# Extra transposes of the identity in front of TensorE's waits

## What is computed

```python
# depth A (d = 1024, 256 tokens)
x = x + gate0 * retention(norm(x) * (1 + scale0) + shift0)      # 4 heads, w_in 1024x6144, w_out 2048x1024
x = x + gate1 * forgetting_attention(norm(x) * (1 + scale1) + shift1)   # 16 heads
x = rms_norm(x, final_g)
# depth B
x = layer_norm(ALPHA * x + conformer_conv(x))      # 31 taps per channel, a layer norm inside
x = layer_norm(ALPHA * x + swiglu(x))              # hidden width 2816
x = layer_norm(ALPHA * x + short_gated_conv(x))    # 3 taps
x = layer_norm(ALPHA * x + mixture_of_experts(x))  # 8 experts, top 2, hidden width 3584
```

## Time and profile before

| | |
|---|---|
| median of 3 runs | 1935.29 us (1934.23 to 1935.48) |
| the profiled execution | 1935.74 us, of which the span of its instructions is 1934.0 us |
| mean granted TensorE clock | 0.974 of full speed |
| TensorE busy with matmuls | 1803.0 us (93% of the span) |
| VectorE, ScalarE, GpSimd busy | 76%, 55%, 2% |
| HBM | 262 GB/s in the mean |

### The profile page before, as it was taken

One profiled execution on the slowest core, in us unless ns is written; L12 is line 12 of the kernel. 1 busy time (PEld: TensorE's weight loads), 2 busy tenths in 40 slices (PEclk: granted clock), 3 DMA queues, 4 the chain that ended last, 5 costly groups with the idle time before them and its releaser, 6 DMA issues.

```text
span 1934.0 us, 23674 instructions
## 1 busy us (share of the span) xinstructions
PE 1803.0 (93%) x9475; PEld 1547.6 (80%) x9475; DVE 1471.2 (76%) x1339; ACT 1062.2 (55%) x912; POOL 34.1 (2%) x34
## 2 busy tenths in 40 slices
PE   2899889988988999897999999999999999999995
PEld 2888678868978998796788887888878888888884
DVE  5686856485976554576788888889888898888895
ACT  1334234553843333232767777767677677777772
POOL 0000002000000000000000000000000000000000
PEclk9999889999999999897999999999999999999998
DMA  9588354405304547454699999999999999999992
GB/s 339 189 301 318 114 214 162 174 14 188 138 1 137 190 153 261 142 186 152 245 339 351 368 366 337 342 354 377 350 342 346 365 361 346 354 361 371 355 380 96
DMA packets 209604, 506.75 MB, mean 262 GB/s; under 512 B 6549, under 2 KB 8877, under 8 KB 209496
## 3 DMA queue, kind: packets, MB, share of 16 engines
q1 hardware_dynamic: 204832, 498.09, 70.6%
q10 hardware_dynamic: 4488, 6.58, 1.0%
q0 software_dynamic: 176, 0.53, 0.1%
HBM read 504.13 MB, written 1.05 MB: 261 GB/s over the span
## 4 chain that ended last, share of the span: by engine, by line
PE 86%; DVE 8%; ACT 2%; issue 2%; DMA 1%; POOL 1%; ACTq 0%; POOLq 0%; DVEq 0%
PE psum L692 27%; PE psum L694 26%; PE psum L693 26%; DVE R L1800 2%; PE psum L1013 2%; PE psum L1041 1%; DVE units L1457 1%; DMA ring<-in_mod_w 1%; POOL root_out L1424 1%; PE psum L1082 1%; DVE stats L1860 1%; DMA R<-in_positions 0%; DVE R L1531 0%; DVE x L1869 0%; PE psum L704 0%
## 5 line engine op out<-in xcount | busy, mean ns | idle before, releaser
L1457 DVE TENSOR_TENSOR units<-ring,units 128x2048 fp32r<-128x2048 f32 x451 | 1012.5, 2278 | 241.0 <-ACT units L1148 167.9
L1365 ACT CAST units<-ring 128x2048 fp32r<-128x2048 f32 x332 | 629.7, 1914 | 244.5 <-PE psum L694 145.9
L692 PE MATMUL psum<-units,xr 128*128 128x512 f32 x1120 | 444.1, 397 | 8.0 <-issue 4.5
L694 PE MATMUL psum<-units,xr 128*128 128x512 f32 x1120 | 438.4, 391 | 0.0
L693 PE MATMUL psum<-units,xr 128*128 128x512 f32 x1120 | 438.1, 391 | 0.0
L1148 ACT CAST units<-ring 128x2048 fp32r<-128x2048 f32 (+1 forms) x119 | 218.4, 1879 | 223.2 <-PE psum L694 187.2
L692 PE MATMUL psum<-units,H 128*128 128x512 f32 x696 | 274.6, 395 | 2.2 <-DVE H L1457 2.2
L694 PE MATMUL psum<-units,H 128*128 128x512 f32 x696 | 272.4, 391 | 0.0
L693 PE MATMUL psum<-units,H 128*128 128x512 f32 x696 | 272.4, 391 | 0.0
L692 PE MATMUL psum<-xr,units 128*128 128x256 f32 x864 | 247.1, 286 | 12.7 <-DVE units L1457 11.4
L692 PEld LDWEIGHTS psum<-units,xr 128*128 128x128 f32 x1120 | 211.6, 189 | 52.7 <-issue 7.6
(11 more groups left out here) (242 smaller groups left out, 1210.0 us busy)
## 6 DMA issues: line engine op xcount, KB each, us to landing
ring<-in_moe_w_gate SPq DMA_DIRECT2D x56, 2048.0 KB, 9.5
ring<-in_moe_w_up SPq DMA_DIRECT2D x56, 2048.0 KB, 9.4
ring<-in_moe_w_down SPq DMA_DIRECT2D x56, 2048.0 KB, 9.6
ring<-in_mod_w SPq DMA_DIRECT2D x12, 2048.0 KB, 9.9
ring<-in_ret_w_in SPq DMA_DIRECT2D x11, 2048.0 KB, 10.1
ring<-in_fox_w_in SPq DMA_DIRECT2D x8, 2048.0 KB, 8.5
ring<-in_sc_w_in SPq DMA_DIRECT2D x6, 2048.0 KB, 7.9
ring<-in_ffn_w_gate SPq DMA_DIRECT2D x5, 2048.0 KB, 8.0
```

What stands on the lines that cost most here:

```text
L692: mm(dst, left[0], right[0], start=first, stop=False)
L694: return mm(dst, left[1], right[0], start=False, stop=last)
L1365: nc.scalar.copy(*expert_unit_parts(q, j, half, 0)).then_inc(unit_high, 1)
L1457: return v.tensor_tensor(dst, src, high.bitcast(F32), ALU.subtract)
```

## The change

`repeat_ident(dst, n)` issues n transposes of the 128x128 identity (the data and the second operand are both the identity) into `dst`. The calls stand in front of waits; the target is a part of a bank that TensorE holds already and whose content the transposes or matmuls behind the wait overwrite. The description of the change speaks of thirteen places; the diff has eleven calls with a count above zero: 10 and 34 in front of heads 1 and 2 of the retention's transposes, 28 in x1T, 32 in x2T, 30 in conf_nT, 36 in front of the second tile of x3T, 38 and 30 in the two tiles of x4T, 36 in front of the second tile of x5T, 22 in front of the rank matmuls and 24 in front of the first gather. That is 320 transposes. In the retention and at the ranks `take_bank` moves ahead of the wait that it followed.

```diff
+            def repeat_ident(dst, n):
+                for _ in range(n):
+                    nc.tensor.transpose(dst, ident, ident)
+
-            def transpose_in(name, src, ready=None):
+            def transpose_in(name, src, ready=None, fill=(0, 0)):
                 banks = [take_bank(name, g) for g in range(4)]
                 for tt in range(NT):
+                    repeat_ident(banks[0][:, tt * P:(tt + 1) * P], fill[tt])
                     if ready is not None:
                         ready(tt)
...
             for h in range(RH):
-                pe.wait_ge(ret_u_ready, 2 * (h + 1))
                 for g in range(2 * h, 2 * h + 2):
                     b = take_bank("ret_uT", g)
+                    if g % 2 == 0:
+                        repeat_ident(b[:, 0:P], (0, 10, 34, 0)[h])
+                        pe.wait_ge(ret_u_ready, 2 * (h + 1))
...
-            transpose_in("x1T", xn1, lambda tt: pe.wait_ge(xn_ready, NT + tt + 1))
+            transpose_in("x1T", xn1, lambda tt: pe.wait_ge(xn_ready, NT + tt + 1), (28, 0))
...
-            transpose_in("x2T", x, lambda tt: pe.wait_ge(x_ready, tt + 1))
+            transpose_in("x2T", x, lambda tt: pe.wait_ge(x_ready, tt + 1), (32, 0))
...
-            transpose_in("conf_nT", conf_n, lambda tt: wait_emptied("conf_cT", 2 * tt + 1))
+            transpose_in("conf_nT", conf_n, lambda tt: wait_emptied("conf_cT", 2 * tt + 1), (30, 0))
...
-            transpose_in("x3T", x, lambda tt: pe.wait_ge(x_ready, NT + tt + 1))
+            transpose_in("x3T", x, lambda tt: pe.wait_ge(x_ready, NT + tt + 1), (0, 36))
...
-            transpose_in("x4T", x, lambda tt: pe.wait_ge(x_ready, NT * 2 + tt + 1))
+            transpose_in("x4T", x, lambda tt: pe.wait_ge(x_ready, NT * 2 + tt + 1), (38, 30))
...
-            transpose_in("x5T", x, lambda tt: pe.wait_ge(x_ready, NT * 3 + tt + 1))
+            transpose_in("x5T", x, lambda tt: pe.wait_ge(x_ready, NT * 3 + tt + 1), (0, 36))
...
+            b = take_bank("rank", 0)
+            repeat_ident(b[:, 0:P], 22)
             pe.wait_ge(mask_ready, 1)
-            b = take_bank("rank", 0)
...
+            repeat_ident(psum[:, 0, 0:P], 24)
             gather(0, 0)
             wide_product(0, 0, 0)
```

## The result

The changed kernel is slower: 1944.16 us median of 11 runs (1941.26 to 1945.69), against 1934.99 for the kernel before in 11 runs beside it. The ratio is 1.0045, with a 95% interval of 1.0034 to 1.0056: 6.6 to 10.8 us. The prediction was 1931.0, a gain, and its range ended at 1936.0.

A forecast was written before the change was run, and what follows sets the result against it. TensorE was taken to bound the kernel (86% of the last chain, VectorE 8%). Terms 1.1 + 1.9 + 0.3 + 0.4 + 1.15 + 0.9 + 0 - 1.5 = 4.25 us gave a median of 1931.0, range 1927.0 to 1936.0.

The forecast's parts named there:

- The experts are untouched and only start sooner: Experts' loop: no term of its own; their transfers are asked for as units come free and move with them.
- as at 1175.4: Inside the experts: starvation that comes and goes by more than 2 us, listed as a sign of being wrong.
- The head: The fills at the nine places up to x5T, without those at the ranks and the gather; terms make 6.05 us.
- Transposes hold the clock: All fills: float32 transposes alone raise TensorE's clock, as seen at x2T, though the Trainium skill says the contrary.
- x1T: Fill of 28: transposes in 1.9 instead of 3.65 us, products at the high clock; 2.6 us in full, 1.9 taken.
- x2T, conf_nT, x1T together: First three seams: gains of 0.3 for x2T, 0.4 for conf_nT (earlier start only) and 1.9 for x1T.
- x3T, x4T, x5T: Later seams: gains of 1.15, 0.9 and 0.3 us; x5T to the ranks taken as 0 altogether, its 0.3 included.
- Retention: Fills of 10 and 34: head 2 delayed 3.6 us under VectorE, products gain between 0 and 2.1; 1.1 taken.
- The ranks: Fill of 22 at the low clock, 4.7 us; x5T to the ranks between -0.5 and +1.7, 0 taken.
- The gather: Fill of 24 before the first gather: 2.0 us later, 0.5 given for the clock; term -1.5, bounds -4.6 and +0.6.
- the slower one: Rival, chance 0.08: fill before the first gather at 912.4 stays at the low clock, gather ends 4.6 us late; 1939.
- Every fill holds: Rival, chance 0.12: clock high at all fills and through L986, 11.7 us gained at most, some 9 likely; 1926.

The follow-up runs named there:

- before_pad56: The kernel before with 56 identity transposes added in a wait near the start, none at the seams: 1943.08 us, ratio 1.0050.
- before_pad72: The kernel before with 72 identity transposes added near the start, none at the seams: 1935.19 us, ratio 1.0008.

## Why the prediction was wrong

**The step that failed** is the sentence "The experts are untouched and only start sooner". Their instructions are untouched, their place in the instruction stream is not. The prediction priced the 320 transposes as time of TensorE and never as code in front of a loop. With the loop put back where it was, the same fills gave a ratio of 0.9979, 4.1 us faster (2.1 to 6.0), against the forecast of 4.25; with them taken out and only the place moved, 13.7 us were lost. The profile of before showed the clue: the idle time at 1175.40 and at 1425.80 is behind the two jumps, both put down to issue. The prediction used these for what idle time does to the clock; it listed starvation "as at 1175.4" that comes and goes among its signs of being wrong, but gave it no term and no rival.

The agreement of 4.1 with 4.25 is in part luck. The head brought 6.2 (4.4 to 8.1) where its terms, x5T's 0.3 with them, make 6.05, and the gather's fill cost 3.1 (1.5 to 4.8) where 1.5 was taken. And the head's own gain is not made where the prediction puts it. In the profiles the changed kernel leads by 3.8 us once the products behind x1T have run at the high clock, loses 1.5 of it from 291.8 on, where its clock fell and that of before did not, and gains 2.8 behind the attention's last short waits, where no fill stands and the clock fell before but not after:
```profile
423.30:429.90 6.60, 5.88 (x20) 4.04 (x19) 4.77 (x8) 4.08 (x3) 0.00 (x0) 0.50 0.01 2
```
```profile
421.00:428.00 7.00, 6.29 (x34) 4.95 (x33) 6.01 (x8) 4.09 (x3) 0.00 (x0) 1.00 0.00 0
```
The first row is before, the second the changed kernel. The same pair, a fall near 294.6 and none at 423, stands in the traces of before_pad56 and before_pad72, which have no fill at any seam. So neither follows from the fills alone, and the prediction has a term for neither.

**Transposes hold the clock**: right, 1.00 through the seams x1T, x2T and x3T.

**x1T**: 1.9 taken, 2.6 in full. In the profile the product comes 4.37 us behind the first transposes instead of 4.81, and the products that were slow run at the high clock, so the full value at the seam; the fall at 291.8 then took 1.5 back. **x2T, conf_nT, x1T together**: terms 2.6, measured 2.3 (0.6 to 4.1), which hides what was said above: from 430 to the first product behind x2T the lead did not grow (4.96 and 4.97 us), where 0.3 was predicted. **x3T, x4T, x5T**: 2.05 for the first two and up to 0.8 through the router; measured 2.3 (0.6 to 4.1).

**Retention**: right in its course. The timeline of the changed kernel, which answers to the earlier trace rows:
```profile
212.09 1.04 PE L869 MATMUL psum<-const,R 128*128 128x128 f32 x8
212.97 1.25 PE L699 MATMUL psum<-const 128*128 128x128 f32 x10
214.06 1.04 PE L869 MATMUL psum<-const,R 128*128 128x128 f32 x8
214.93 3.88 PE L699 MATMUL psum<-const 128*128 128x128 f32 x34
218.64 1.04 PE L869 MATMUL psum<-const,R 128*128 128x128 f32 x8
220.90 1.06 PE L869 MATMUL psum<-const,R 128*128 128x128 f32 x8 [1.22 <-DVE R L1683]
223.63 0.77 PE L692 MATMUL psum<-units,H 128*128 128x512 f32 x1 [1.67 <-DVE H L1467]
```
The ten had no wait to fill, head 2 came at 218.64 instead of 215.75 (219.3 was predicted), and the product still followed the start of head 3 by about the old distance, 2.73 us against 2.83. Its first eight products were at the low clock all the same, from 223.6 to 227.0, so of the 2.1 that were possible about 0.8 came (5.4 against 6.2 us for the head, inside the error).

**The ranks**: the router's matmuls kept part of the high clock (5.70 us instead of 7.00), as predicted, and the 22, expected at the low clock in 4.7, ended at the high one, in 3.92. What they are worth the timed runs do not tell (0.9978 with them, 0.9968 without, the intervals overlap).

**The gather**: 2.0 for the fill predicted, 2.35 in the profile that has it alone, 3.1 (1.5 to 4.8) in the timed runs.

**The rivals**: the slower one named the right sign and the wrong place. The clock did fall in gaps that the fills leave, for one stretch of 3.4 us each at the retention's products and at x4T. "Every fill holds" was nearly so up to the router; at the router the clock fell, as was expected.

## What to carry to other kernels

Instructions added in front of a loop move the loop within the pieces in which code is fetched. Where it began a few instructions before the end of a piece, each jump back cost 6.3 us more here, some 4.3 of them idle and most of the rest the low clock behind it, however little the instructions themselves cost. Look for idle time put down to "issue" a few instructions behind a jump. Sixteen instructions more ahead of the loop cured it here (72 transposes instead of 64), sixteen fewer did so only in part (8.6 us of 13.4 stayed). When an edit ahead of such a loop is measured, the loop should keep its place. A fill in a wait pays only if it stands ahead of the late semaphore: behind it, as in front of the gather, it is on the path.

## What the runs showed of the hardware

Behind a jump TensorE can go on with the second piece of instructions 5.4 to 5.9 us after it went on with the first (two jumps in each of three kernels), though one packet took only 1.0 to 1.1 us to move. The DMA engines were busy for 0.93 of the time there (the row of 1172.00:1177.61); whether that traffic has a part in the distance, no run shows.

In the changed kernel the clock fell in a place where before it had not, while TensorE was busy without a gap. The first row is that of small products of the attention (32 and 16 columns), the second that of the full-width products right behind them:
```profile
288.80:291.50 2.70, 2.70 (x27) 2.70 (x26) 1.55 (x3) 2.70 (x2) 0.97 (x2) 1.00 1.05 410
291.60:294.70 3.10, 3.10 (x9) 2.43 (x9) 2.44 (x2) 0.77 (x1) 0.60 (x1) 0.54 0.26 94
```
The granted clock is 1.00 in the first and 0.54 in the second. The same fall behind the same products is in before_pad56 and before_pad72 (0.50 from 294.80 on), not in the kernel before; why it comes in some kernels only is open.
